# Latent attention on TensorE: the values matmuls and the heads' turns move to the slots of the scores

## The reference

```
q_nope, q_pe = qB[..., :128], rope(qB[..., 128:], pos)        # 128 and 64 columns per head
k_nope, vB   = kvB[..., :128], kvB[..., 128:]
s = (q_nope @ k_nope.T + q_pe @ k_pe.T) * scale               # causal
o = softmax(s) @ vB
```

## Time and profile before

| | |
|---|---|
| median of 3 runs | 1639.9 us (1638.22 to 1641.71) |
| the profiled execution, its own time | 1644.14 us |
| span of the profiled execution | 1642.3 us |
| TensorE (PE) busy | 1620.0 us, 99% of the span |
| VectorE (DVE), ScalarE (ACT), GpSimd (POOL) busy | 51%, 50%, 41% |
| granted TensorE clock, mean | 0.999 |
| the two bodies of the latent attention | about 1037 to 1205 us |

### The profile page before, as it was taken

The page is one execution under the profiler, slowest core; times in us unless marked ns, Lnnn a source line. Parts: engine busy times, 40 slices in busy tenths (PEclk is TensorE's granted clock), DMA queues, the critical chain, the costliest instruction groups (busy, mean ns, idle before and its releaser), DMA issues.

```text
span 1642.3 us, 22656 instructions
## 1 busy us (share of the span) xinstructions
PE 1620.0 (99%) x8343; PEld 1344.9 (82%) x8343; DVE 845.1 (51%) x1934; ACT 819.8 (50%) x1759; POOL 675.8 (41%) x569
## 2 busy tenths in 40 slices
PE   9999999999999999999999999999999999999998
PEld 7788898888888887888888887888877777878886
DVE  3346656564213756467545451432245455767674
ACT  3346666765333454454445456444456565344561
POOL 4453434334666700667110124644444335655022
PEclk9999999999999999999999999999999999999999
DMA  6454546455778877857998947745554414624762
GB/s 220 131 154 99 159 91 183 94 148 111 175 176 197 231 224 226 269 154 203 243 258 252 241 140 264 230 129 141 152 162 102 132 53 144 141 100 129 244 243 103
DMA packets 139595, 281.13 MB, mean 171 GB/s; under 512 B 11051, under 2 KB 19052, under 8 KB 139324
## 3 DMA queue, kind: packets, MB, share of 16 engines
q1 hardware_dynamic: 86012, 160.29, 29.9%
q0 software_dynamic: 31664, 81.70, 24.2%
q10 hardware_dynamic: 21808, 37.68, 7.2%
HBM read 254.68 MB, written 92.06 MB: 211 GB/s over the span
## 4 chain that ended last, share of the span: by engine, by line
PE 90%; DVE 4%; ACT 2%; issue 2%; POOL 1%; DMA 1%; POOLq 0%; ACTq 0%; DVEq 0%
PE acc L686 17%; PE acc L688 17%; PE acc L687 17%; PE turn L783 3%; PE acc L827 2%; PE acc L826 2%; PE acc L828 2%; PE turn L1122 2%; PE turn L828 2%; PE turn L827 2%; PE turn L826 2%; PE sc L828 2%; PE sc L827 2%; PE sc L826 2%; PE turn L708 2%
## 5 line engine op out<-in xcount | busy, mean ns | idle before, releaser
L1808 POOL TENSOR_TENSOR w_lo<-w_raw,w_hi 128x512 fp32r<-128x512 f32 x341 | 507.6, 1497 | 723.9 <-ACT w_hi L1238 723.0
L1238 ACT ACTIVATE w_hi<-w_raw 128x512 fp32r<-128x512 f32 x565 | 353.2, 628 | 432.1 <-PE acc L688 233.0
L686 PE MATMUL acc<-w_hi,setA_hi 128*128 128x512 f32 (+1 forms) x1088 | 443.9, 408 | 6.5 <-DVE setA_lo L2007 3.1
L688 PE MATMUL acc<-w_hi,setA_lo 128*128 128x512 f32 (+1 forms) x1088 | 421.5, 387 | 0.0
L687 PE MATMUL acc<-w_lo,setA_hi 128*128 128x512 f32 (+1 forms) x1088 | 420.2, 386 | 0.0
L686 PEld LDWEIGHTS acc<-w_hi,setA_hi 128*128 128x128 f32 x1088 | 205.2, 189 | 44.8 <-issue 6.1
L688 PEld LDWEIGHTS acc<-w_hi,setA_lo 128*128 128x128 f32 x1088 | 204.5, 188 | 42.6
L687 PEld LDWEIGHTS acc<-w_lo,setA_hi 128*128 128x128 f32 x1088 | 205.7, 189 | 29.7
L2199 DVE TENSOR_TENSOR w_lo<-w_raw,w_hi 128x512 fp32r<-128x512 f32 x224 | 155.5, 700 | 143.5 <-ACT w_hi L1238 143.2
L1323 ACT ACTIVATE p_w<-sm,negm 128x256 f32<-128x256 f32 (+1 forms) x128 | 60.6, 474 | 56.5 <-DVE sink_d L2076 56.5
L1645 ACT ACTIVATE p<-sm,negm 128x144 f32<-128x144 f32 (+3 forms) x96 | 54.3, 565 | 52.3 <-DVE negm L2510 34.4
(11 more groups left out here) (519 smaller groups left out, 3108.2 us busy)
## 6 DMA issues: line engine op xcount, KB each, us to landing
w_raw<-in_swa_w_in SPq DMA_DIRECT2D x35, 1024.0 KB, 7.5
w_raw<-in_w_in SPq DMA_DIRECT2D x32, 1024.0 KB, 5.6
w_raw<-sum_out SPq DMA_DIRECT2D x64, 256.0 KB, 4.3
sum_k<-in_w_in POOLq DMA_DIRECT2D x24, 512.0 KB, 7.0
sum_out<-in_swa_w_out POOLq DMA_DIRECT2D x24, 512.0 KB, 7.7
sum_v<-in_w_in POOLq DMA_DIRECT2D x24, 512.0 KB, 9.0
w_raw<-in_w_in SPq DMA_DIRECT2D x48, 256.0 KB, 5.4
sum_out<-in_w_out POOLq DMA_DIRECT2D x24, 512.0 KB, 6.6
```

The lines of the kernel that those rows point to most:

```text
L686: mm(acc[t][:, 0:cols], hi[:, kc, rows], wh, start=(k == 0), stop=False)
L688: last = mm(acc[t][:, 0:cols], lo[:, kc, rows], wh, start=False, stop=(k == K - 1))
L1238: nc.scalar.activation(w_at(f)[0], raw_of(f), ACT.Copy).then_inc(done, 1)
L1808: nc.gpsimd.tensor_tensor(lo, raw_of(f), hi.bitcast(F32), ALU.subtract).then_inc(s_lo, 1)
```

## The change

Two numbers of the schedule change, for the latent attention alone.

```diff
-                self.turn_after, self.values_after = (3, 5) if self.mla else (4, 6)
+                self.turn_after, self.values_after = (3, 6) if self.mla else (4, 6)
...
-            return 12 * head + ((2, 5, 7)[b] if A.mla else (2, 5)[b])
+            return 12 * head + ((3, 6, 9)[b] if A.mla else (2, 5)[b])
```

## The result

The changed kernel takes 1652.5 us (median of 4 runs, 1649.4 to 1653.4) against 1640.8 us for the kernel before (4 runs, 1638.2 to 1641.7). The ratio is 1.007, with a 95% interval of 1.0055 to 1.0085: slower. The forecast was 1650.5 us, in a range of 1646 to 1656. It added 10.6 us to the 1639.9 us of three runs; a fourth run of the kernel before has moved that median to 1640.8.

What follows compares the result with a forecast made beforehand. TensorE, busy 99% of the span, was taken to bound the kernel, its changes moving the end one for one. Added waits of 12.7 us less 2.1 removed gave +10.6, from 1639.9 to 1650.5 us, range 1646 to 1656.

Steps and rivals of the forecast that it cites:

- turn b = 0: Heads 1 to 3, two bodies: the turn of p behind it waits for ACT's copy, 0.17 us six times, 1.0 us.
- turn b = 1: Heads 1 to 3, two bodies: the turn of p behind it waits for DVE's copy, 0.64 us six times, 3.8 us.
- turn b = 2: Heads 1 to 3, two bodies: it waits for `keep_o2` of the values issued immediately ahead, 0.72 us six times, 4.3 us.
- first unit of a head: Slots 24, 36, 48, two bodies: turn of p waits for `keep_o2` of its slot's values, 0.27 us six times, 1.6 us.
- slot 60: Once per body: no scores left between values and turn of p, a wait of 0.70 us twice, 1.4 us.
- end: End of the second body: L1159 waits for the last values, now directly ahead; 0.6 us, once.
- removed: 38 group boundaries 0.2 us, twelve waits for ACT's copies 1.7 us, one wait for the rotation 0.2 us: 2.1 us.
- the wait for `keep_o2`: TensorE waits for DVE's copy of the values: 0.72 us at head turns, 0.27 at first units, 0.70 where no scores are left.
- The clock: Rival: new waits beside transposes lower TensorE's granted clock; a tenth of the stretch adds 9 us, total about 1659; 2%.
- Chained waits: Rival: late softmax delays `keep_o2` on DVE and the turns waiting for it; six delays add 5 us, total 1656; 13%.
- Partly covered: Rival: copies begin earlier, so the new waits are partly covered; +3.3 to +8.5 us, around 1646; 8%.
- A cost per switch: Rival: hidden cost of switching between plain fp32 and fp32r, deciding from 0.28 us per group; at 0.4 us, 1635.5 us; 4%.

## Why the prediction was right

The mechanism is as forecast, and so are its places but for two small ones. Term by term, measured in the changed kernel's trace with the same landmarks:

| term | predicted, us | measured, us |
|---|---|---|
| turn b = 0, six times | 0.17 each, 1.0 | 0.19 each, 1.14 |
| turn b = 1, six times | 0.64 each, 3.8 | 0.59 each, 3.54 |
| turn b = 2, six times | 0.72 each, 4.3 | 0.80 each, 4.80 |
| first unit of a head, six times | 0.27 each, 1.6 | 0.34 each, 2.04 |
| slot 60, twice | 0.70 each, 1.4 | 0.78 each, 1.56 |
| scores of 272 columns with no turn b = 0, twice | covered, 0 | 0.06 each, 0.12 |
| end | 0.6 | 0.52 |
| added | 12.7 | 13.7 |
| removed | 2.1 | 2.4 (13.7 - 11.3) |
| sum | +10.6 | +11.3 |

The first unit and slot 60 in the changed kernel:

```profile
1080.91 0.41 PE L1071 MATMUL sc<-knT,qnT 128*128 128x144 f32 x2
...
1081.68 0.27 PE L1108 MATMUL turn<-ident,p 128*16 128x128 f32 x1 [0.18 <-DVE o_nat L2528]
...
1117.60 0.39 PE L1123 MATMUL turn<-natm_v,pTm 128*128 128x128 f32 x2
...
1118.60 0.27 PE L1108 MATMUL turn<-ident,p 128*16 128x128 f32 x1 [0.61 <-DVE o_nat L2528]
```

For the end, the last L1123 starts at 1212.66 and L1159 at 1213.38, 0.72 later instead of 0.11, and 0.09 of that was paid before.

*The mis-sized term is the wait for `keep_o2`* (0.72, 0.27 and 0.70, against 0.80, 0.34 and 0.78). Its length was copied from a place where `keep_o2` had one semaphore to wait for. The prediction did see that it now comes behind the reciprocal, but priced that only as a chain of late softmax. There was no such chain: the reciprocal is done long before, and DVE idles 1.48 us ahead of `keep_o2`. What costs is that place in the order, with its second wait: 0.07 us, 14 times, 1.0 us; taking it away gave 0.8 back. It also uncovers two places that the prediction called covered by 0.01 us: L1108 behind scores of 272 columns at 1106.19, 0.77 us behind L1071 and not 0.71, and once more in the second body. That the total came so close owes something to luck, since turn b = 1 was off the other way.

*Turn b = 1* came out 0.05 shorter, since DVE's copy started 0.07 sooner behind the last transpose: 1070.70 - 1069.77 = 0.93 against 1089.17 - 1088.17 = 1.00 in the earlier trace rows.

*The removed part* rests on more than the subtraction. Taking away the six waits behind turn b = 2 alone gave 0.8 us, against 6 x 0.14 = 0.84. The trace of the kernel before says the same of both halves. At all six places of turn b = 2, L1040 starts 0.32 us behind L688 where 0.23 is usual, and its second start follows 0.16 later where 0.11 is usual: 0.14. For the six values behind it L1122 starts 0.27 behind L688 and spans 0.10 too much, again 0.14:

```profile
1092.42 0.39 PE L688 MATMUL acc<-w_hi,setA_lo 128*128 128x512 f32 x1
1092.69 0.71 PE L1122 MATMUL turn<-nat_v,pT 128*128 128x128 f32 x4
```

In the changed kernel, where they do not wait for knT, the same four matmuls last 0.60 us (the row at 1073.90). A group boundary at 0.005 us, 0.1 us for 18 more groups, fits the 0.2 measured; the stretch is not measured well enough to say more.

*The rivals.* The clock stays at 1.00 over a window with 9.27 us of idle TensorE, so the case for the lower level is closed for this kernel; the Trainium skill's rule on transposes ("TensorE: Matmul & The Clock Gate", Part 4: PE-mode transpose), by which they do not count as TensorE activity as matmuls do, changed nothing that the granted clock shows. Chained waits: none, each wait has the length of its own turn's copy (two copies at turn b = 1) or of `keep_o2`. Partly covered: no. A cost per switch: refuted by the kernel with 18 more groups.

*What the prediction said would be seen*, waits of the loads for qpT, qnT and o_nat by name, was seen in part. The loads' waits have the right counts (20 and 6) and lengths, but are put down to "issue". The matmuls' waits name o_nat as forecast. For qpT and qnT the copies had to be found in the timeline. And L1040 still has two waits for DVE's qpT, as before, which belong to head 0.

## What to carry to other kernels

Before you merge small work into fewer, larger groups, list for each instruction in it which buffer it waits for and what runs between the last use of that buffer and it: the projection that seemed to interrupt the fp32 work was the cover of three different copies, and 11 us of waits stand against some 0.2 us of boundaries saved. When two edits are made together, look for a wait that needs both (here six, 4.8 us). Where one engine waits for a short copy on another, look at what stands directly in front of that copy and count its own semaphores: here a second one was collected earlier, by an instruction that is not urgent, and 0.8 us came back.

## What the hardware showed beyond that

- `keep_o2` on DVE starts 0.07 us later (0.38 to 0.39 against 0.31 to 0.32) where it has a second semaphore to wait for, directly behind a reciprocal, although DVE had been idle for 1.48 us and the reciprocal was done. This holds at the places of both kernels that have the extra instruction, and at none of the others.
- Alternating plain fp32 and fp32r matmuls costs next to nothing: +0.2 us for 18 more groups in 165.7 us, about 0.01 us each.
- The step from the end of a copy to the start of the matmul that waits for it is not one number per engine. It is 0.15 us from `keep_o2` on DVE to L1040 (1075.18 to 1075.33) and to L1108 (1115.32 to 1115.47 in the earlier trace rows), and 0.10 from DVE's qpT to L1108 (1071.39 to 1071.49). From ACT it is 0.10 to L1108 (1066.62 to 1066.72) and 0.06 to L1040 (1091.06 to 1091.12 in the earlier trace rows). Why `keep_o2` is slower than the other copy of the same engine was not tested and stays open.
- 26 waits beside fp32 transposes, in which weight loads idled up to 0.8 us and matmuls up to 0.61, 9.27 of 179 us in all, did not lower the granted clock.
